# One decoder step: a new opening, and page compression in ten pieces over three buffers

## The reference

```python
def compress_blocks(rows, pe, w1, w2):
    b, l, g, d = rows.shape
    z = rows.reshape(b, l // BLOCK, BLOCK, g, d) + pe[None, None, :, None, :]
    z = jnp.transpose(z, (0, 1, 3, 2, 4)).reshape(b, l // BLOCK, g, BLOCK * d)
    return jax.nn.silu(z @ w1) @ w2
# nsa_sample: fc = full_rows(cache_cmp, kv_c)      (8 samples x 16 pages, gathered by page_table)
kc = compress_blocks(fc[:, :, 0], cmp_pe[0], cmp_w1[0], cmp_w2[0])
vc = compress_blocks(fc[:, :, 1], cmp_pe[1], cmp_w1[1], cmp_w2[1])
```

## Time and profile before

| | us |
|---|---|
| median of 3 runs | 1705.39 (1701.01 to 1705.9) |
| the profiled execution, whole | 1708.29 |
| its span, first to last instruction | 1706.6 |
| PE busy in the span | 1609.1 (94%) |
| DVE, POOL, ACT busy | 807.2, 563.7, 550.4 |

### The profile page before, as it was taken

The page is one execution under the profiler, slowest core; times in us unless marked ns, Lnnn a source line. Parts: engine busy times, 40 slices in busy tenths (PEclk is TensorE's granted clock), DMA queues, the critical chain, the costliest instruction groups (busy, mean ns, idle before and its releaser), DMA issues. The chain is left out here.

```text
span 1706.6 us, 40632 instructions
## 1 busy us (share of the span) xinstructions
PE 1609.1 (94%) x16686; PEld 1499.4 (88%) x16686; DVE 807.2 (47%) x1350; ACT 550.4 (32%) x1040; POOL 563.7 (33%) x505
## 2 busy tenths in 40 slices
PE   6999987999989999999998899999989999999996
PEld 5998975566679999999998799889889999999995
DVE  4333114666647443443138677666447444433235
ACT  3110003555545222222234433323344222222242
POOL 0001222676724433443015243333014444343013
PEclk9999778999999999999999999999989999999998
DMA  8654687977451223323243234333231222223242
GB/s 267 230 190 171 207 314 276 368 246 252 148 186 63 75 86 88 96 86 116 99 148 124 66 121 137 89 113 100 75 101 49 87 86 96 89 87 118 98 157 84
DMA packets 86264, 238.50 MB, mean 140 GB/s; under 512 B 18109, under 2 KB 20847, under 8 KB 84545
## 3 DMA queue, kind: packets, MB, share of 16 engines
q1 hardware_dynamic: 80786, 221.63, 39.0%
q0 software_dynamic: 3392, 11.02, 1.8%
q10 hardware_dynamic: 1936, 3.74, 0.7%
HBM read 217.81 MB, written 23.77 MB: 142 GB/s over the span
## 5 line engine op out<-in xcount | busy, mean ns | idle before, releaser
L846 DVE TENSOR_TENSOR layer_w_lo<-ring,layer_w_hi 128x1024 fp32r<-128x1024 f32 (+1 forms) x138 | 225.5, 1634 | 266.1 <-ACT layer_w_hi L728 266.1
L993 PE MATMUL layer_ps<-layer_x_hi,layer_w_hi 128*128 128x260 f32 x1312 | 268.5, 284 | 3.8 <-DVE layer_w_lo L846 2.7
L993 PE MATMUL layer_ps<-layer_x_hi,layer_w_lo 128*128 128x260 f32 x1312 | 267.8, 284 | 0.0
L993 PE MATMUL layer_ps<-layer_x_lo,layer_w_hi 128*128 128x260 f32 x1312 | 267.3, 283 | 0.0
L728 ACT ACTIVATE layer_w_hi<-ring 128x1024 fp32r<-128x1024 f32 (+1 forms) x138 | 161.0, 1168 | 222.6 <-PE layer_ps L993 206.4
L993 PE MATMUL layer_ps<-layer_h_lo,layer_w_hi 128*128 128x260 f32 x960 | 217.9, 287 | 11.0 <-DVE layer_h_lo L852 11.0
L993 PEld LDWEIGHTS layer_ps<-layer_x_hi,layer_w_hi 128*128 128x128 f32 x1312 | 204.1, 189 | 5.3 <-DVE layer_w_lo L846 2.9
L993 PEld LDWEIGHTS layer_ps<-layer_x_hi,layer_w_lo 128*128 128x128 f32 x1312 | 204.2, 189 | 0.0
L993 PEld LDWEIGHTS layer_ps<-layer_x_lo,layer_w_hi 128*128 128x128 f32 x1312 | 203.5, 189 | 0.1
L993 PE MATMUL layer_ps<-layer_h_hi,layer_w_hi 128*128 128x260 f32 x704 | 172.8, 286 | 4.8 <-DVE layer_w_lo L846 4.8
L993 PEld LDWEIGHTS layer_ps<-layer_h_lo,layer_w_hi 128*128 128x128 f32 x960 | 160.9, 192 | 12.0 <-DVE layer_w_lo L846 11.8
(11 more groups left out here) (323 smaller groups left out, 2969.1 us busy)
## 6 DMA issues: line engine op xcount, KB each, us to landing
ring<-in_w_gu SPq DMA_DIRECT2D x88, 512.0 KB, 3.5
ring<-in_w_down SPq DMA_DIRECT2D x48, 704.0 KB, 4.0
arena<-in_cache_cmp SPq DMA_DIRECT2D x86, 256.0 KB, 5.4
ring<-in_hgrn_w_in SPq DMA_DIRECT2D x32, 512.0 KB, 4.0
ring<-in_nsa_w_in SPq DMA_DIRECT2D x21, 512.0 KB, 5.4
arena<-in_cache_cmp POOLq DMA_DIRECT2D x42, 256.0 KB, 5.7
kv_slot<-in_slc_kv SPq DMA_DIRECT2D x32, 256.0 KB, 4.9
arena<-in_slc_kv SPq DMA_DIRECT2D x32, 256.0 KB, 4.4
```

What stands on the lines that cost most here:

```text
L846: dve.tensor_tensor(self.w_lo[slot][:, 0:kcs * P], c.ring[:, s, 0:kcs * P], self.w_hi[slot][:, 0:kcs * P].bitcast(F32), ALU.subtract).then ...
L993: mm = pe.matmul(bank[:, h, 0:TH], wt[slot][:, a], xt[:, x, COLS[h]], start=start and part == 0, stop=stop and part == 2)
```

## The change

*Opening.* The block `bias_rows` is gone, and an object `Opening` puts its work inside `linear`. SP now issues norm weights, tile 0, x in eight slices with a semaphore each, then tiles 1 to 3. ACT issues the small loads, runs one throw-away activation, and cuts slice k of x once that slice is there. The two bias products go to PE between the units 1 and 2, into the bank of unit 3; DVE scales them and ACT stores them there. The 5.2 MB transfer is cut into eight of two heads each, beside the tiles of the steps 2 to 5 and 7 to 10.

*Compression.* The pieces have 16, 16 and 8 pages in turn, three times, and 8 at the end: ten in all. The third buffer is `at.slots[2]`, 8 pages of the attention's keys (`kv_slot`). Its first load waits for nothing. The last piece lies in the second half of buffer 0; `slots[3]`, a window bank, is its first half, and SP loads it right after the bias tiles. PE's other work is spread anew between the pieces. `kv_out` is stored later. The last two `far` products stand after the last piece, and their copies on ACT after the SiLU.

*Hand-over.* The last root of layer 0 is taken by ACT after the cut of the first tile's high part, not before it.

```diff
+SPREAD_STEPS = (2, 3, 4, 5, 7, 8, 9, 10)
...
+                if isinstance(i, int) and i == 0 and s == 2 and opening is not None:
+                    opening.rows(eng, ps[RING - 1])
...
+                    if eng is nc.scalar:
+                        first.last_root(eng)
...
+                if s == 2 and opening is not None:
+                    opening.tensor(pe, ps[RING - 1])
...
-        end.root(act, 4, COLS[1])
...
+    def sync(self, sp):
+        c, d = self.c, self.d
+        sp.dma_start(c.nw[:, :, :, :], d["norm_w"]).then_inc(self.norm_in, 16)
+        load_tile(sp, c, d["nsa_w_in"], 0, 0, KC)
+        for k in range(KC):
+            sp.dma_start(c.X[:, k, :], d["x"][:, k, :]).then_inc(self.x_in[k], 16)
+        for s in range(1, RING):
+            load_tile(sp, c, d["nsa_w_in"], s, s, KC)
+        sp.wait_ge(self.pages_in, 16)
+    def scalar(self, act):
+        c, d = self.c, self.d
+        act.dma_start(self.oh, d["onehot_rows"][:, 0]).then_inc(self.rows_in, 16)
+        act.dma_start(self.tabs[:, :], d["tabs"]).then_inc(self.rows_in, 16)
+        act.dma_start(c.pages[:, :], d["page_table"]).then_inc(self.pages_in, 16)
+        for dst, src in self.small:
+            act.dma_start(dst, d[src]).then_inc(self.loaded, 16)
+        act.wait_ge(self.ones_made, 1)
+        act.activation(c.scrap[:, :], c.ones[:, 0:1], ACT.Copy)
+        act.wait_ge(self.norm_in, 16)
...
+    def tensor(self, pe, bank):
+        pe.wait_ge(self.rows_in, 32)
+        for j in range(2):
+            pe.matmul(bank[0:16, j, :], self.tabs[:, 0:16], self.oh[:, j * 512:(j + 1) * 512], start=True, stop=True)\
+              .then_inc(self.made, 1)
+    def rows(self, eng, bank):
+        c = self.c
+        if eng is c.nc.vector:
             for j in range(2):
-                pe.matmul(ps[j][0:16, :], tabs[:, 0:16], oh[:, j * 512:(j + 1) * 512], start=True, stop=True)\
-                  .then_inc(made, 1)
-        @block.vector
-        def _(dve):
-            for j in range(2):
-                dve.wait_ge(made, j + 1)
-                dve.tensor_scalar(R[:, j * 512:(j + 1) * 512], ps[j][0:16, :], HD ** 0.5, None, ALU.mult).then_inc(moved, 1)
+                eng.wait_ge(self.made, j + 1)
+                eng.tensor_scalar(self.R[:, j * 512:(j + 1) * 512], bank[0:16, j, :], HD ** 0.5, None, ALU.mult)\
+                   .then_inc((self.moved, c.psum_free[RING - 1])[j], 1)
+        if eng is c.nc.scalar:
+            eng.wait_ge(self.moved, 1)
+            eng.wait_ge(c.psum_free[RING - 1], 1)
+            eng.dma_start(self.d["bias_scratch"], self.R).then_inc(self.row_out, 16)
...
+        sizes = [CH, CH, half] * turns + [half]
+        first_page = [sum(sizes[:g]) for g in range(len(sizes))]
+        LAST = len(sizes) - 1
+        rows = [in_arena(0, CH), in_arena(CH, CH), at.slots[2]]
+        rows_of = lambda g: in_arena(half, half) if g == LAST else rows[g % 3]
+        taken = lambda g: g // 3
+        SHARE = {CH: ((0, 9), (9, 7)), half: ((0, 5), (5, 3))}
+        landed = lambda g, who: 16 * sum(SHARE[sizes[x]][who][1] for x in range(g % 3, g + 1, 3) if x >= 2)
...
+            first, count = SHARE[sizes[g]][who]
+            if taken(g):
+                eng.wait_ge(chunk_done[g % 3], taken(g))
             for x in range(first, first + count):
-                page = eng.value_load(c.pages[0:1, g * CH + x:g * CH + x + 1], min_val=0, max_val=POOL - 1)
-                eng.dma_start(slot(g % 2)[:, x, :], d["cache_cmp"][bass.ds(page, 1)].rearrange("o p n -> p (o n)"))\
-                   .then_inc(rows_in[who][g % 2], 16)
+                at_page = first_page[g] + x
+                page = eng.value_load(c.pages[0:1, at_page:at_page + 1], min_val=0, max_val=POOL - 1)
+                eng.dma_start(rows_of(g)[:, x, :], d["cache_cmp"][bass.ds(page, 1)].rearrange("o p n -> p (o n)"))\
+                   .then_inc(rows_in[who][g % 3], 16)
...
+            load_chunk(sp, 2, 0)
...
+            load_chunk(sp, 3, 0)
...
-            for g in range(3, NCH):
+            for g in range(4, LAST + 1):
                 load_chunk(sp, g, 0)
-            sp.wait_ge(skew_out, 16)
+                if g == 5:
+                    sp.dma_start(d["kv_out"], HT[:, CK_U:GATE_U, :]).then_inc(kv_saved, 16)
+            sp.wait_ge(skew_out, 16 * len(SPREAD_STEPS))
             load_bias_tiles(sp, d, at, 0)
+            sp.dma_start(at.slots[3], d["win_kv"][0]).then_inc(at.slot_in[3], 16)
+            sp.wait_ge(chunk_done[2], turns)
             sp.dma_start(at.slots[2], d["win_kv"][WIN_BANKS - 1]).then_inc(at.slot_in[2], 16)
...
+                out = slice(first_page[g] * 4, (first_page[g] + sizes[g]) * 4)
                 if g >= 2:
                     for who in range(2):
-                        pe.wait_ge(rows_in[who][s], 16 * SHARE[who][1] * (g // 2))
+                        pe.wait_ge(rows_in[who][g % 3], landed(g, who))
                 for kv in range(2):
                     for t in range(TP):
                         for g2 in range(2):
                             col = kv * 256 + t * 8 + g2 * 4
-                            mm = pe.matmul(ps_c[kv][g2 * HD:(g2 + 1) * HD, g * CH * 4:(g + 1) * CH * 4], w1[:, kv, t, :],
-                                           slot(s)[:, :, col:col + 4], start=t == 0, stop=t == TP - 1)
-                mm.then_inc(chunk_done[s], 1)
+                            mm = pe.matmul(ps_c[kv][g2 * HD:(g2 + 1) * HD, out], w1[:, kv, t, :],
+                                           rows_of(g)[:, :, col:col + 4], start=t == 0, stop=t == TP - 1)
+                mm.then_inc(chunk_done[g % 3], 1)
```

More of the change, by code:

```diff
@@ L134, in repeat, with linear @@
             yield i
-def linear(c, name, w, n_units, subs, kcs, src, evac, nxt, scale=None, beside=None, norm=None, early=None, late=None, work=None, unrolled=False, first=None, start=0):
+def linear(c, name, w, n_units, subs, kcs, src, evac, nxt, scale=None, beside=None, norm=None, early=None, late=None, work=None, unrolled=False, first=None, start=0, opening=None):
     nc = c.nc
@@ L243, in _ @@
         def _(sp):
+            if opening is not None:
+                opening.sync(sp)
             if first is not None:
@@ L297, in root @@
                 act.activation(c.rstd[:, :], c.rstd[:, :], ACT.Sqrt).then_inc(rooted, 1)
+            if opening is not None:
+                opening.scalar(act)
             if first is not None:
@@ L371, in _ @@
         def _(pool):
+            if opening is not None:
+                opening.gpsimd(pool)
             if post is not None:
@@ L417, in add_squares @@
                 pe.wait_ge(squared, k + 1)
+                if opening is not None and k == 0:
+                    pe.wait_ge(opening.ones_made, 1)
                 token_sums(ps[2], sq[:, k % 2, :], k == 0, k == kcs - 1).then_inc(added, 1)
@@ L931, in vector, with last_root @@
         end.mean(dve, own_end, 1)
+    def last_root(self, act):
+        self.end.root(act, 4, COLS[1])
     def rooted(self, dve):
@@ L1282, in _ @@
         def _(pool):
-            for g in range(2, NCH):
+            for g in range(2, LAST + 1):
                 load_chunk(pool, g, 1)
@@ L1322, in far, with block_bias, block_scores @@
                           start=True, stop=True).then_inc(far_biased, 1)
+            def block_bias():
+                pe.wait_ge(onehots, 32)
+                for x in range(PBLK + 2 * (TILES - 1)):
+                    first = BLOCK * (2 * (TILES - 1) - x) - (BLOCK - 1) + 511
+                    mm = pe.matmul(b[2][:, x * 16:(x + 1) * 16], oh[:, first:first + P], tabs[:, 0:16], start=True, stop=True)
+                mm.then_inc(blocks_biased, 1)
+            def block_scores():
+                pe.wait_ge(bias_out, 1)
+                pe.wait_ge(kc_ready, 1)
+                for i in range(TILES):
+                    for u in range(8):
+                        col = (i * 8 + u) * 16
+                        mm = pe.matmul(b[2][:, col:col + 16], c.XW[:, u, i * P:(i + 1) * P],
+                                       kcBD[:, u // REP].rearrange("p g n -> p (g n)"), start=True, stop=True)
+                mm.then_inc(scores, 1)
             pe.wait_ge(w1_in, 16)
@@ L1334, in _ @@
             mm.then_inc(new_turned, 1)
+            chunk(1)
             pe.wait_ge(pairs_ready, 1)
             prompt(0)
+            chunk(2)
             prompt(1)
-            pe.wait_ge(onehots, 32)
-            for x in range(PBLK + 2 * (TILES - 1)):
-                first = BLOCK * (2 * (TILES - 1) - x) - (BLOCK - 1) + 511
-                mm = pe.matmul(b[2][:, x * 16:(x + 1) * 16], oh[:, first:first + P], tabs[:, 0:16], start=True, stop=True)
-            mm.then_inc(blocks_biased, 1)
+            chunk(3)
+            pe.wait_ge(small, 32)
+            pe.wait_ge(prompt_out, 2)
+            pe.matmul(b[0][:, 0:16], w2[:, 0, :], hid[:, 0, 512:528], start=True, stop=True).then_inc(second, 1)
+            block_bias()
+            chunk(4)
             values(0, b[5])
```

(21 more changed lines are left out.)

106 lines of the change are left out of this document (48 added, 58 removed).

## The result

The changed kernel takes 1721.95 us (median of 10 runs, 1710.34 to 1726.26) beside 1703.31 us for the kernel before (10 runs, 1698.83 to 1707.67): 1.0093 times as long, interval 1.0072 to 1.0114. It is slower by some 18.6 us, where 1697.7 us had been predicted. The profiled execution took 1718.16 us, of which 1716.5 are span.

A forecast was written before the change was run, and what follows sets the result against it. PE bounds the projection; time could come back at the start and in the compression, where PE waits and runs slowly. Opening -7.7, bias products +0.5, compression +0.5 and hand-over -1.0 sum to -7.7 us: 1697.7 us, range 1683 to 1710.

The forecast's parts named there:

- the clock term: In the compression, 11 us lost to low clock in place of 20, small pieces at full clock: -9.1 us (-17 to 0).
- opening (first product): At the start, PE's first projection matmul at 8.3 us instead of 15.99: -7.7 us (bounds -6.1 and -8.0).
- row products (projection): Between units 1 and 2, two bias products come onto PE's path, partly in an existing wait: +0.5 us (0 to +2.1).
- two more pieces at full clock: In the compression, ten pieces for eight, a small one costing 7.68 us like a full one: +15.4 us.
- wait for pages: In the compression, PE's 5.09 us wait ahead of the seventh piece goes, as loads start earlier: -5.1 us.
- `cmp_w2` late: In the compression, SP issues it behind five page loads, delaying DVE's layout of the prompt's pairs: +0.5 us (0 to +4).
- `far`, SiLU, last products: At the compression's end, the last `far` products fill part of PE's 2.12 us wait for the SiLU: -1.2 us.
- gaps of issue: In the compression, gaps inside pieces while DMA engines were full were left unchanged: 0 (between -6 and +5).
- hand-over: After layer 0's last root, DVE starts right behind it because ACT's cut comes first: -1.0 us (0 to -1.05).
- first rival: In the compression, a small piece costs half, or the clock holds nearly everywhere: 1682 us in all; chance 0.12.
- price of a small piece: In the compression, a piece of 8 pages at 32 columns takes 7.68 us, as long as one of 16.
- third rival: In the compression, small pieces don't hold the clock, 6.3 us each: 1717 to 1723 us with three or four; chance 0.13.

The follow-up runs named there:

- the two runs: Kernel before with new opening and hand-over: eight pieces in two buffers with the new order of thin work, 1685.85 us (0.9909); with the old compression, 1691.27 us (0.9926).
- the run with narrow pieces: Kernel before, with every product but the first of a sum streaming 32 columns instead of 64 in all eight pieces: 1743.99 us, ratio 1.0165.
- the compression alone: Kernel before with only the new compression (ten pieces, three buffers, new order), behind the old opening and hand-over: 1728.78 us, ratio 1.0162.

## Why the prediction was wrong

One step failed, the clock term: the prediction had pieces of 32 columns at full clock, and three of four ran at 1.2 GHz for most of their length. Measured from the two profiles, us, by PE's rows:

| term | predicted | measured |
|---|---|---|
| opening (first product) | -7.7 | -7.4 (8.58 for 15.99) |
| row products (projection) | +0.5 | +0.3 (133.4 for 133.1) |
| two more pieces at full clock | +15.4 | +15.4 |
| wait for pages | -5.1 | -5.1 |
| `cmp_w2` late | +0.5 | 0 here; 1.0 and 1.7 in two runs |
| `far`, SiLU, last products | -1.2 | 0 (wait -2.1, slower products +2.2) |
| gaps of issue | 0 | +2.0 (10.9 for 8.9) |
| clock | **-9.1** | **+14.4** |
| hand-over | -1.0 | -1.05 |

The rows of the compression sum to 26.7; its length grew by 25.7, since neighbouring rows overlap a little. In the prediction's own numbers two slips change nothing: 11 in place of 20 is -9.0, not -9.1, and the range from 1683 leaves out the first rival's 1682.

*The price of a small piece was right.* At full clock piece 5 took 8.1 us, 31 ns a record, for 32 columns, a full one 7.7. This is the rule of the Trainium skill, TensorEngine Tiling (Array Packing), Instruction Overhead, that a product of one column takes as long as one of sixty. The trace agrees at 32 columns, which no run had shown before.

*The clock was mis-sized, with its sign.* The prediction put 9 us back, by priced recoveries for the prompt, the bias and the waits, and nothing lost in the small pieces. Measured: the four small pieces lose 17.8 us (48.5 for 4 times 7.68); the bias and the value transposes give back 3.7; the prompt nothing (12.9 us as before: its first half slowed behind a gap of 2.11 us, its second began behind a slow piece); the scores +0.5, the full pieces -0.3. That the narrow columns are the cause is shown by the two edits that change columns alone: twice the columns took 13 us off, half of them added 28. The third rival had this at 13 chances in 100, and its price of 6.3 us for each slow piece was near: 6.2, 5.0 and 6.3. Its 1717 to 1723 us for three or four hold the measured 1722, but with some luck: it named the prompt's lost recovery beside them without a price. What spoke for it stood in the earlier trace rows: 17 columns at 0.50 for 11 us without a rise, though PE never stood still in them. The prediction read there that the clock fell "after PE had stood still or worked on few columns", priced the pieces as if they weren't work on few columns, and dismissed it with the argument that 32 columns fill the array for twice as long. No row bore on that choice, and the term that it decided was larger than the forecast gain.

*The order of the thin work gave back less than 9.1 us with full pieces.* With eight of them the compression is 9.6 us shorter in the profiles (120.8 for 130.4 us). That this is near the 9.1 put down for the clock is chance: by the rows PE's own work gives back some 5 us of it, the prompt 4.4 and the bias 2.4, while the full pieces lose 2.4; the gaps of issue are 6.1 us shorter (5.2 for 11.3), and the waits for pages 2.9 longer. A second profile of this kernel, on another chip, has 124.5 us, with 9.0 of gaps. By time the two runs stand at 0.9909 and 0.9926 of the kernel before with intervals that overlap, so what the order alone is worth isn't shown. Shown are the opening's gain, and that the third buffer, which removed one wait of 5.1 us, cost two pieces (15.4) and their clock (17.8).

## What to carry to other kernels

When a change splits work into narrower products, price the instruction count first and then ask at which clock the narrower ones run: between 17 and 64 columns the time per product didn't follow the columns here, but the clock could. A row where few columns run slowly though PE is always busy is the warning. Before thin work is moved out of the way of dense work, see which loads it was hiding.

## What was not expected of the hardware

- PE can be busy without a gap and stay at 1.2 GHz: 24.6 us from 264.10 us on in the changed kernel, at 0.50 to 0.51, and 133 us, from 172 to 305, in the run with narrow pieces. The Trainium skill, TensorE: Matmul & The Clock Gate, What's actually happening, says that "activity releases the throttle"; a PE that was always busy did not do so in these stretches, and the measurement decides.
- The same 32 columns can keep full speed or come back to it: piece 5 ran at 1.00, narrow pieces behind the projection did for 9.37 us, and piece 2 in the compression alone rose from 0.50 to 1.00 within some 4 us.
- Wider products are not enough by themselves: the scores went from 16 to 64 columns and ran at 0.50 all the same, and took no less time.
- The fall isn't the same for the same products: piece 2 took 13.85 us in the changed kernel and 9.4 us behind the old opening, one profile of each; the changed kernel's runs spread over 16 us. What decides it from run to run was not tried.
- The stretch behind the compression varied between 1417 and 1435 us over profiles and chips, and the mean clock of the recurrence between 0.95 and 0.98; a gain of some us there can't be read from one profile.
